# Expert gathers of a two-block kernel: a row of v asked for eight experts behind its row of u, in place of four

## What is computed

```python
def peer_ffn(xm, w_query, sub_keys, expert_u, expert_v):
    def one_block(xblk):                       # 128 tokens
        q = (xblk @ w_query).reshape(B, TOKEN_BLOCK, N_PEER_HEADS, 2, SUBKEY_DIM)
        s = jnp.einsum('bthpd,hpnd->bthpn', q, sub_keys).astype(jnp.float32)
        vals, idx = lax.top_k(s, PEER_TOPK)    # 16 of 128 keys, twice
        ...
        top_s, pos = lax.top_k(cand, PEER_TOPK)
        eidx = jnp.take_along_axis(cand_idx, pos, axis=-1)
        g = jax.nn.softmax(top_s, axis=-1).astype(xblk.dtype)
        u = expert_u[eidx]
        h = jnp.einsum('btd,bthkd->bthk', xblk, u)
        act = jax.nn.gelu(h, approximate=False) * g
        return jnp.einsum('bthk,bthkd->btd', act, expert_v[eidx])
```

## Time and profile before

| | |
|---|---|
| median of three runs | 3691.03 us (3689.93 to 3694.55) |
| the profiled execution, its own time | 3692.66 us |
| its span | 3690.8 us |
| PE busy | 3245.5 us, 88% |
| DVE busy | 2385.4 us, 65% |
| ACT busy | 1455.3 us, 39% |
| POOL busy | 1100.7 us, 30% |
| expert stage of layer 1 (282 to 1041 us) | 759 us, 378 GB/s, DMA share 0.98 |
| expert stage of layer 2 (1292 to 2048 us) | 756 us, 377 GB/s, DMA share 0.98 |

### The profile page before, as it was taken

How to read it: one execution, slowest core, us unless ns; L and a number is a source line. 1 busy time by engine, 2 the same in 40 slices (tenths; PEclk the granted TensorE clock), 3 DMA queues, 4 the chain that set the end, 5 groups by cost and what they waited for, 6 DMA issues and landing times. The chain is left out here.

```text
span 3690.8 us, 50838 instructions
## 1 busy us (share of the span) xinstructions
PE 3245.5 (88%) x18906; PEld 2578.2 (70%) x18906; DVE 2385.4 (65%) x4712; ACT 1455.3 (39%) x2866; POOL 1100.7 (30%) x1211
## 2 busy tenths in 40 slices
PE   6997998777779979987676899999999999999999
PEld 5895554222268955543222798898899998898899
DVE  7775766665667546666665566877566657767665
ACT  3642222221246412222222444565454544665543
POOL 1305666666613056666666000000000000000000
PEclk8998999888899989988888999999999999999999
DMA  8669999999976499999999554444355554343454
GB/s 298 215 220 337 409 409 376 366 368 378 366 263 206 139 347 409 408 375 370 370 373 364 185 183 145 136 132 137 121 184 185 182 182 137 132 138 130 134 187 161
DMA packets 258290, 937.14 MB, mean 254 GB/s; under 512 B 29312, under 2 KB 30720, under 8 KB 257792
## 3 DMA queue, kind: packets, MB, share of 16 engines
q0 software_dynamic: 161280, 587.27, 41.7%
q1 hardware_dynamic: 96768, 346.62, 28.1%
HBM read 932.73 MB, written 1.05 MB: 253 GB/s over the span
## 5 line engine op out<-in xcount | busy, mean ns | idle before, releaser
L710 PE MATMUL M<-rows,diag 128*128 128x512 f32 x2048 | 989.0, 634 | 263.9 <-issue 197.6
L710 PEld LDWEIGHTS M<-rows,diag 128*128 128x128 f32 x2048 | 401.0, 202 | 810.4 <-issue 745.8
L268 DVE TENSOR_TENSOR w_low<-ring,w_high 128x1024 fp32r<-128x1024 f32 x560 | 686.3, 1228 | 415.8 <-ACT w_high L260 413.1
L287 PE MATMUL G<-x_high,w_high 128*128 128x256 f32 x2576 | 762.0, 296 | 51.4 <-DVE w_low L268 18.4
L290 PE MATMUL G<-x_high,w_low 128*128 128x256 f32 x2576 | 739.0, 287 | 0.0
L260 ACT ACTIVATE w_high<-ring 128x1024 fp32r<-128x1024 f32 x560 | 589.3, 1056 | 348.1 <-PE G L287 324.3
L289 PE MATMUL G<-x_low,w_high 128*128 128x256 f32 x2448 | 704.0, 288 | 0.0
L414 POOL DMA_INDIRECT rows<-in_expert_v_dram,expert x512 | 483.4, 944 | 343.6 <-issue 126.0
L414 POOL DMA_INDIRECT rows<-in_expert_u_dram,expert x512 | 483.8, 945 | 322.3 <-DVE expert L1207 146.6
L287 PEld LDWEIGHTS G<-x_high,w_high 128*128 128x128 f32 x2576 | 505.0, 196 | 64.9 <-issue 39.7
L290 PEld LDWEIGHTS G<-x_high,w_low 128*128 128x128 f32 x2576 | 505.2, 196 | 0.0
(11 more groups left out here) (363 smaller groups left out, 4985.0 us busy)
## 6 DMA issues: line engine op xcount, KB each, us to landing
ring<-in_stream_dram SPq DMA_DIRECT2D x654, 512.0 KB
ada_ring<-in_ada_stream_dram POOLq DMA_DIRECT2D x80, 512.0 KB, 4.8
rows<-in_ada_stream_dram POOLq DMA_DIRECT2D x16, 512.0 KB
rows<-in_expert_u_dram,expert POOLq DMA_INDIRECT x512
rows<-in_expert_v_dram,expert POOLq DMA_INDIRECT x512
const<-in_const_dram SPq DMA_DIRECT2D x1, 1096.5 KB, 11.1
x<-in_x_dram SPq DMA_DIRECT2D x1, 1024.0 KB, 5.3
out_dram<-x SPq DMA_DIRECT2D x8, 128.0 KB, 3.3
```

Source lines behind the costliest of these rows:

```text
L268: dve.tensor_tensor(T["w_low"][:, part, :], T["ring"][:, place.slot(chunk, slots), :], T["w_high"][:, part, :].bitcast(F32), ALU.subtract) ...
L287: mm = pe.matmul(out, T["w_high"][:, part, tile], high(k), start=(k == 0), stop=False)
L710: mm = pe.matmul(M[:, 2 * t + half, :], T["diag"][:, n % 4, :], T["v_rows"][:, n % SLOTS, half * 512:(half + 1) * 512], start=(h == 0 and ...
```

## The change

`behind`, by which the gathers of v trail those of u in POOL's queue, goes from SUB (4) to SLOTS (8). All semaphore waits keep their values; PE, DVE, ACT and SP have the same instructions in the same order.

```diff
-            experts, behind = ROUNDS * TOPK, SUB
+            experts, behind = ROUNDS * TOPK, SLOTS
             for n in range(experts + behind):
                 if n < experts:
                     r, k = divmod(n, TOPK)
```

## The result

| | before | after |
|---|---|---|
| median (four runs each) | 3691.74 us (3689.93 to 3694.55) | 3752.18 us (3750.06 to 3764.80) |
| ratio after to before, 95% interval | | 1.0170 (1.0146 to 1.0194) |
| the profiled execution, its own time | 3692.66 us | 3764.80 us |
| its span | 3690.8 us | 3763.0 us |

The change makes the kernel 60 us slower, 1.7%, where +24 was predicted.

The account below looks back on a forecast made before the run. It took memory to bound rounds 2 to 5 and a late `v_used` signal to hold the second half. 2 x (0 + 5 + 8) - 1.9 = +24.1 us on 3691.0 gave 3715 us, range 3660 to 3760.

Parts of the forecast that it names:

- Rounds 1 to 6, the key scores: First half of each stage: DVE's routing waits for key scores behind PE's v rows; +5 us a layer, between 0 and 24.
- the 6.4 us to spare: Rounds 2 to 5: POOL's spare time per round against the memory, said to pay for most of a 4 us wait.
- Start: Stage start: four gathers left for later against v(8) to v(15) no longer waiting; 0, between -5 and +5 us a layer.
- Second half, weights: Later rounds: DVE's weighting waits for diagonals behind later v rows; +8 us a layer, between -24 and +30.
- The signs: Second half: POOL's waits for DVE over 20 us a stage, for PE and "remote" falling, DVE's L1240 waiting longer for gelu.
- The over 100 us a stage: Sign in the expert stages: DVE's L1240 waits for ACT's gelu many times longer, over 100 us a stage.
- End: Behind the last u: eight v rows remain, but that u comes 5.0 us sooner; -1.9 us together, between -8 and +8.
- Only the end counts: Rival, stage end: v simply later, four more rows behind the last u; +10 us, 3701 us; chance 0.07.
- Faster: PE is freed of DVE: Rival, second half: diagonals come early, PE's waits for them go; 3665 us, or 3644 with half POOL's waits gone; chance 0.28.
- No change: Rival: memory in the first half and the late signal in the second set the pace; 3691 us; chance 0.22.
- The key scores close the loop in every round: Rival: none of 4 us a round absorbed in six rounds, second half at its upper bound; +108, 3799 us; chance 0.05.
- The window that I had said would stay within 3 us of 185: Sign that the forecast is right: the time of rounds 2 to 5, 185.1 us before, stays within 3 us of 185.

Follow-up runs that it names:

- the second pair of profiles: The change and the kernel before, unaltered, each profiled again on a run where the kernel before is slow: 3758.17 and 3691.99 us.
- kind B: Runs, of either kernel or an edit, in which the kernel before takes 3588 us and POOL never waits on a "remote" signal; change against before 3596.10 to 3587.60 us.
- a lag of six: v gathers six experts behind u, against the kernel before with four: 3690.79 against 3693.55 us, ratio 0.9993.
- kind A: Runs, that of the result among them, in which the kernel before takes 3692 to 3694 us; change against before measured again 3756.68 to 3693.55 us.
- the early copy: The change with ACT's key-score copy behind the third group of diagonals instead of the fourth, against the kernel before: +88.7 us, ratio 1.0238, where before is slow.

## Why the prediction was wrong in size

**The step that failed** is the last part of *Rounds 1 to 6, the key scores*: "POOL waits about 4 us a round in a new place. PE catches up by as much while it does, and the 6.4 us to spare pay for most of it ... I take 0.8 us a round". The new loop is 4.9 us longer than the round (51.2 less 46.3), and none of that was absorbed: +28.8 and +27.0 us a layer, above its upper bound of 24. The 6.4 us to spare were POOL's, against the memory. The new loop doesn't go through POOL's spare time: every event in it, row 16r-9 among them, is asked for at a fixed distance from u(16r), so a later u(16r) moves the whole chain and the next one can't catch up. POOL and the memory stand while it closes (373 GB/s in place of 408). A loop longer than the round sets the round.

The loop's length was nearly right, 50.4 us against 51.1, but by two errors that cancel. Routing was to begin 29.8 us behind u(16r), and begins at 33.2: the chain passes through the weighting ahead of it (late signal, gates, gelu, weighting, four diagonals, copy), which I had put under the second half only. From there to the numbers I had 17.6 us, which is what it takes (17.5), and 3 us for late signals on DVE's own chain, which don't come there.

**Start**: 0 predicted, within -5 and +5; -10.1 and -10.3 measured. POOL now stands for expert 3 from an earlier point, with u(11) asked for at 312.07 instead of 316.17 us, and the waits for `v_used` behind it are gone: u(16) is 9.3 us ahead. I had set the four gathers left for later against that. They come later indeed, but in rounds that the loop paces.

**Second half, weights**: +8 predicted, +11.4 and +9.1 measured, +7.8 and +8.6 in the second pair of profiles. The signs are the named ones: POOL waits for DVE 30.6 us (3.0 before), for PE 16.0 (20.6) and "remote" 25.8 (36.9); DVE's L1240 stands longer for gelu (groups of instructions of after, 633 to 1050 us):

```profile
L1240 DVE SCALAR_TENSOR_TENSOR weight<-gelu,gate_inv,gate 128x4 f32<-128x4 f32 x35 | 7.7, 220 | 51.3 <-issue 30.1 <-ACT gelu L921 20.9
```

This was 27.6 us. The over 100 us a stage that I had named are there with the 91.7 of rounds 1 to 6.

**End**: -1.9 for both layers, bounded by -8 and +8. In it stood 23.3 us from the last u to the end of PE's last row, less 5.0 us because the last u was to come four gathers sooner. The table measures from the last u, and there 23.3 stands against 27.4 and 27.1 us: +8.1 for both layers in the table's terms, where +16.0 was measured (27.4 less 22.1 and 27.1 less 16.4). In layer 2 the last nine rows run without a gap, as I had it, but they begin 9.7 us behind the last u, after a wait for ACT's diagonal, in place of 7.5, and take 1.93 us each in place of 1.75. The 5.0 us never came: the second half, in which a sooner last u would show, is longer. On kind B the end takes longer (35.6 us), with the last v asked for at 976.84 us and used from 990.99, and PE's last three rows each wait for their v; there the loss a layer is 2.7 to 5.3 us, and the whole change costs 8.5. The Trainium skill's rule ("DMA: Bandwidth & Descriptors", Rules for kernel authors), to issue a DMA early and wait late, was the better guide to its sign. Its rival, "Only the end counts", gave +10.

**The rivals.** *Faster: PE is freed of DVE* fell, though its premise came true: PE's waits for diagonals in the second half went from 13.1 to 2.0 us, and brought nothing: PE then waited for rows (38.5 us for landing v rows, 10.5 before). Its second figure was also summed wrong: 3665 less half of POOL's 47 us in each layer is 3618, not 3644. *No change* fell. *The key scores close the loop in every round* was the mechanism of the first half, for which I gave 0.05; its 24 us a layer was nearer than my 5, its 30 for the second half too much. The window that I had said would stay within 3 us of 185 is 204.8, which shows the same.

Slower by over 0.2% was the likeliest side, and 3752 us lies in the range, near its upper end. That it does is partly luck: in the profiles the first half's loop cost +55.8 us where I had +10, and the start, which I had at 0, gave back 20.4 of it.

## What to carry to other kernels

Where a change makes a producer run ahead, follow every chain that starts at an event and comes back to the same event one round later, add up all that stands in it on each in-order engine, also what is merely queued ahead, and compare the sum with the round. Here a lag of six, below it, was free; with a lag of eight, above it, the whole excess was paid in each round, and another engine's spare time didn't pay for it. Before moving one link of such a chain forward, see what it will then stand in front of: on kind A the early copy cost 26 us more although it removed the wait it was meant to remove.

## What the hardware showed that was not expected

The two kinds differ by 104 us, 2.8%, on the same kernel, and by a factor of seven in what the change costs (63.1 and 8.5 us). On kind A a use of a row by PE reaches ACT some 6 us late in rounds 2 to 6 of the change, at the same place, and POOL has "remote" waits of up to 4.8 us; in the profiles of kind B POOL and ACT have none. The record doesn't say what makes a run of the one kind or the other: chip number 9 gave both. What is behind it wasn't found: the records of PE's matmuls are the same length on both (3.60 us for two rows), and their ends are modelled, so whether PE is late or only its signal can't be told. On kind A PE stood 5.37 us behind them and then ran 16 matmuls in 3.76 us instead of 1.95, at a granted clock of 0.50 (1.2 GHz; 1.00 on kind B, 2.4 GHz). The mean granted clock of the change's profile is 0.942 there and 0.977 on kind B. That late signals make the difference of the two kinds is what the rows show side by side, and isn't shown as the cause; no run changed the signals alone.

Two table loads of 1.28 us each stand in the loop between the late signal and gelu, since the gates' exp and gelu take turns. The Trainium skill ("ScalarE activation tables: per-element evaluation and per-set limits", What a function is on this engine) puts two functions of different sets one load of 1283 ns apart, and the rows agree. Moving them out of the chain wasn't tried.
